# Gate rows ahead of the first projection's last chunk, their bias on VectorE, the sigmoid table loaded there, buffers cleared on GpSimd, and TensorE without a barrier into the attention

## The chip, the core and the metric

One program on one core of a Trainium2 chip (trn2). The metric is the device time of one execution in microseconds, the median of several; lower is better. Of the engines, PE is TensorE, ACT is ScalarE, DVE is VectorE, POOL is GpSimd, and SP is SyncE, which here only issues DMAs. ACT issues DMAs as well, on a queue of its own (q10; SP's is q1).

## What is computed

One layer of a hybrid encoder block: an adaptive norm of `x`, one combined input projection, a stick-breaking attention branch (8 heads of 64), a gated DeltaNet branch (4 heads of 128), sigmoid merge gates, an output projection and a gated residual. S = 1024 rows, D = 1024. The parts that the change touches:

```python
mod = silu(c) @ ada_w + ada_b
shift, scale, gate = split(mod, 3)
h = rms_norm(x, norm_g) * (1 + scale) + shift
p = h @ w_in                     # sb_q, sb_k, sb_v, sb_z, dn_*, merge_*
qa = rms_norm(heads(sb_q), sb_q_g); ka = rms_norm(heads(sb_k), sb_k_g); va = heads(sb_v)
o_sb = stick_breaking_attention(qa, ka, va) * silu(sb_z)
...
out = x + gate * (y @ w_out)
```

For a block of 128 queries, stick-breaking attention takes `keep = sigmoid(-z)` of the scores, a running product of `keep` from the diagonal back over the keys, and weighs differences of neighbouring value rows with it.

## The kernel before

All five engines run written-out instruction streams, ordered by semaphores. The program is a list of phases. At the end of phases 1 and 2 (and 3, but for TensorE) each engine drains, raises `phase_end` and waits until all five have (`end_phase`, L252): a barrier. Phase 1 is the first projection, phase 2 the attention.

**Phase 1** (`pe_1`, `act_1`, `dve_1`, `pool_1`, `sp_1`). 1536 columns of `w_in` (q, k, v of the attention) go in NCH = 6 chunks of 256, the last with 8 columns more. A chunk is 8 row tiles (ST); a tile is 24 matmuls, as each factor is split in a high and a low part and three of the four products are taken (`three`, L266 to L268). ACT copies every tile from PSUM to `rows` and raises `r_ok`. DVE sums squares for the norms of q (part 0) and k (part 1); ACT makes `y1` from them with Ln and Exp (L638, L639), the second time behind the copy of the last chunk's fourth tile; DVE then scales all eight row tiles (`normalize`, L663, L667), and makes the high part of a first weight tile `w3hl` of the next projection (L740), from which POOL makes the low part (L747). The per-channel gate of the residual: DVE sums `ada_w` weighted by silu(c) into `gacc` (128 x 1024), and a product with a matrix of ones sums over partitions and spreads the row over all of them; a second product adds the bias row `adab`. This stands behind the last chunk:

```python
for half in range(2):
    nc.tensor.matmul(bank(5 + half), ones[:], gacc[:, ...], start=True, stop=False)        # L619
    t = nc.tensor.matmul(bank(5 + half), ones[0:1, :], adab[0:1, ...], start=False, stop=True)   # L620
t.then_inc(gate_mm, 1)
```

ACT copies the result to `gate` (L641) as its last work of the phase.

**Phase 2** (`pe_2`, `act_2`, `dve_2`, `pool_2`, `sp_2`). PE first turns k and q of the first pair of heads (`turn(0)` to `turn(3)`, 16 transposes, L954), then works 24 matmuls of the next projection (`fill_2(-1)`, L758), then `scores(0)` and `scores(1)` (L971, L973). ACT casts the turned blocks (`high`, L1038) and DVE makes the low parts (`low`, L1091). The k half is copied by DMA to the other 64 partitions (`second_half`, the DMA `qk<-qk`, L924, two of them, semaphore `dup_ok`); `scores(0)` waits for it. SP writes the value rows to DRAM (`v_scratch<-rows`, L918, 2 MB) and, when they have landed, reads back the last row of each tile (`vE`, L929, `e_in`) and all rows shifted by one (`vsh`, L930, 2 MB, `v_in`). PE turns vE (L1014) between `scores(1)` and `scores(2)`, and DVE copies that to `vTe` (L1109) between scans 0 and 1. POOL takes `vsh - v` in four instructions (L1124, `dv_ok`), which the weighted sums (`values`, L1000) and later `high(4)` need.

The attention has 64 steps n, a query block of one head each, with the longest key range first: 1024, 1024, 896, 896, 768, 768, 640, 640, ... columns. A step is: scores on PE, `keep(n)` on ACT (sigmoid, L1045), `scan(n)` on DVE (the running product, L1098), transposes on PE (`flips`, L985), copies on ACT (L1053), and `values` on PE. PE's order is written out: `scores(0)`, `scores(1)`, vE's transposes, `scores(2)`, the 24 matmuls of `fill_2(0)`, `scores(3)`, `flips(0)`, and so on.

Of the kernel before, what the change touches and what calls it, by code (L numbers as in the profile page):

```python
# [26 lines left out]
P = 128  # L27
# [23 lines left out]
def hybrid_block(nc, x, c, ada_w, ada_b, norm_g, w_in, sb_q_g, sb_k_g, conv_w, dn_a_log, dn_dt_bias,  # L51
# [21 lines left out]
    with ctx:  # L73
# [213 lines left out]
        ss1_ok, y1_ok = sem("ss1_ok"), sem("y1_ok")  # L287
# [312 lines left out]

        def pe_1(pe):
            first_chunks(pe)
            for ch in range(2, NCH):
                pe.wait_ge(w1_hi, ch + 1)
                pe.wait_ge(w1_lo, ch + 1)
                for st in range(ST):
                    n = (ch - 1) * ST + st
                    pe.wait_ge(r_ok, n - 2 if ch == 2 and st < 4 else n - 3)
                    for kt in range(KT):
                        w = [t[:, kt, 0:width_1(ch)] for t in (high_of(ch), low_of(ch))]  # L610
                        t = three(bank(n % 4)[:, 0:width_1(ch)], hhi[:, kt, P * st:P * st + P],
                                  hlo[:, kt, P * st:P * st + P], w[0], w[1], kt == 0, kt == KT - 1)
                    t.then_inc(r_mm, 1)

            pe.wait_ge(r_ok, ST)
            pe.wait_ge(gacc_ok, 1)
            pe.wait_ge(par1_in, 80)
            for half in range(2):
                nc.tensor.matmul(bank(5 + half), ones[:], gacc[:, 512 * half:512 * half + 512], start=True, stop=False)  # L619
                t = nc.tensor.matmul(bank(5 + half), ones[0:1, :], adab[0:1, 512 * half:512 * half + 512],  # L620
                                     start=False, stop=True)
            t.then_inc(gate_mm, 1)

        def act_1(act):
# [4 lines left out]
            for n in range(ST, (NCH - 1) * ST):  # L629
                ch, st = n // ST + 1, n % ST  # L630
                act.wait_ge(r_mm, n + 1)
# [8 lines left out]
            act.wait_ge(gate_mm, 1)  # L640
            nc.scalar.copy(gate[:], psum[:, 5:7, :].rearrange("p a b -> p (a b)"))  # L641

        def dve_1(dve):
# [13 lines left out]
            def normalize(part):  # L657
# [3 lines left out]
                for st in range(ST):  # L661
                    v = rows[:, part, st].rearrange("p (h d) -> p h d", d=HD)
                    t = nc.vector.tensor_tensor(v, v, rstd1[:, st, :, None].to_broadcast([P, SBH, HD]), ALU.mult)  # L663
                    if part:

                        link(dve, dve_chain, t)
                        nc.vector.tensor_tensor(v, v, gain[:, 2, None, :].to_broadcast([P, SBH, HD]), ALU.mult)  # L667
# [12 lines left out]
            dve.drain().then_inc(gacc_ok, 1)  # L680
# [236 lines left out]
        def sp_2(sp):  # L917
            sp.dma_start(v_dram[1:1 + S].rearrange("(t p) n -> p t n", p=P), rows[:, 2]).then_inc(vd_out, 16)  # L918
# [28 lines left out]
        def pe_2(pe):  # L947
            def turn(u):

                part, half = TURNS[u % 4]  # L950
                if u >= 4:
                    pe.wait_ge(fl_ok, u - 1)
                for j in range(4):
# [4 lines left out]
            def scores(n):  # L958
                pair, qb, head = steps[n]
                if n % PER == 0:  # L960
                    pe.wait_ge(fl_ok, 4 * pair + 3)
                    pe.wait_ge(dup_ok, 32 * (pair + 1))
# [42 lines left out]

            for u in range(4):
                turn(u)
            fill_2(pe, -1)
            pe.wait_ge(c2_ok, 2)
# [18 lines left out]
        def act_2(act):  # L1028
            act.preload_act_table_set("sigmoid_and_others")
# [54 lines left out]
        def dve_2(dve):  # L1084
# [16 lines left out]
            nc.vector.memset(cast(qk[HD:P, 0, 2]), 0.0)  # L1101
            nc.vector.memset(floor[:, 0:S - P], 0.0).then_inc(c2_ok, 1)
# [15 lines left out]
        def pool_2(pool):  # L1118
            nc.gpsimd.memset(cast(qk[HD:P, 1, 2]), 0.0).then_inc(c2_ok, 1)
            pool.wait_ge(v_in, 16)  # L1120
            pool.wait_ge(c2_ok, 2)
# [896 lines left out]
        def run(eng, *phases):  # L2018

            for n, phase in enumerate(phases):  # L2020
                phase(eng)
                if n in (1, 2) or n == 3 and eng is not nc.tensor:
                    end_phase(eng, n)
                elif n == 3:
# [35 lines left out]
```

## Time and profile before

| | us |
|---|---|
| median of 3 runs | 1000.46 (998.68 to 1000.68) |
| profiled execution, its time | 1000.31 |
| its span in the trace | 998.4 |
| PE busy | 960.5 (96%) |
| DVE busy | 526.7 (53%) |
| ACT busy | 321.2 (32%) |
| POOL busy | 194.2 (19%) |

The trace is one execution, with times from the start of its span; 1.9 us of its time lie outside the span. Phase 1's last chunk ends at about 177 us, and phase 2 lasts from 182 to 338 us. TensorE's clock has two levels, 1.2 and 2.4 GHz; the views give the granted one as a share of the upper, and its mean over this execution is 0.987. In the chain of waits each step is the work, or the transfer, that released the next.

### The profile page before, as it was taken

The page shows a single profiled execution, that of the slowest core. Times are in us where ns is not written, and L with a number is a line of the kernel's source. Part 1 is how long each engine was busy: PE and PEld are TensorE (multiplying, and loading weights), DVE is VectorE, ACT ScalarE, POOL GpSimd, SP SyncE. Part 2 cuts the span into 40 slices and gives each one's busy share as a digit, 9 for nine tenths or more (in the row PEclk, how much of TensorE's full clock was granted, in tenths as well). Part 3 has the DMA queues.
Part 4 walks back from the last instruction along what each step waited for, and adds up shares of the span by engine and source line. Part 5 has one row for each costly group of instructions (what it writes and reads, how often), then busy time and mean ns, then how long its engine had stood idle before and what let it go on. Part 6 is the DMA issues. An engine that isn't in the chain of part 4 may idle for free.

```text
span 998.4 us, 14136 instructions
## 1 busy us (share of the span) xinstructions
PE 960.5 (96%) x5731; PEld 806.6 (81%) x5731; DVE 526.7 (53%) x763; ACT 321.2 (32%) x732; POOL 194.2 (19%) x96
## 2 busy tenths in 40 slices
PE   4999999999999899999999999999999989999998
PEld 3889999677777688888887888888888768787886
DVE  3776895689777245544233357123335456754422
ACT  7552111477876322112541111122322642110000
POOL 0001120160001011221222121100010026773000
PEclk9799999899999999999999999999999999999999
DMA  9851500611210211111312434512112773436231
GB/s 320 234 172 42 171 2 22 213 42 27 62 46 15 60 50 53 43 43 43 94 55 85 125 107 132 123 43 74 54 43 74 263 253 127 147 106 211 90 100 64
DMA packets 120587, 100.58 MB, mean 101 GB/s; under 512 B 18023, under 2 KB 100544, under 8 KB 120266
## 3 DMA queue, kind: packets, MB, share of 16 engines
q1 hardware_dynamic: 90218, 76.07, 25.3%
q10 hardware_dynamic: 30304, 23.60, 7.9%
q8 instruction: 46, 0.75, 0.3%
q14 instruction: 19, 0.16, 0.1%
HBM read 73.44 MB, written 24.12 MB: 98 GB/s over the span
## 4 chain that ended last, share of the span: by engine, by line
PE 77%; DVE 7%; DMA 6%; ACT 4%; POOL 3%; issue 2%; SPq 1%; ACTq 0%; DVEq 0%
PE psum L758 36%; PE psum L266 8%; PE psum L268 7%; PE psum L267 7%; DMA sg<-z_scratch 3%; DVE stick L1098 3%; PE psum L1000 3%; PE psum L985 2%; PE psum L971 1%; PE psum L1325 1%; ACT sg L1899 1%; POOL hlo L1928 1%; POOL sg L1937 1%; POOL w3hl L747 1%; PE psum L381 1%
## 5 line engine op out<-in xcount | busy, mean ns | idle before, releaser
L758 PE MATMUL psum<-hhi,w3hl 128*128 128x512 f32 x1120 | 370.5, 401 | 5.1 <-issue 2.3
L758 PEld LDWEIGHTS psum<-hhi,w3hl 128*128 128x128 f32 x1120 | 211.6, 189 | 50.9 <-issue 5.6
L758 PE MATMUL psum<-hlo,w3hl 128*128 128x512 f32 x560 | 219.2, 391 | 0.0
L747 POOL TENSOR_TENSOR w3hl<-w3raw,w3hl 128x1024 fp32r<-128x1024 f32 x43 | 104.6, 2432 | 510.3 <-DVE w3hl L740 510.3
L758 PEld LDWEIGHTS psum<-hlo,w3hl 128*128 128x128 f32 x560 | 106.1, 189 | 21.8 <-issue 1.9
L1098 DVE TENSOR_TENSOR_SCAN stick<-stick,floor 128x1024 f32<-128x1024 f32 (+7 forms) x64 | 94.2, 1510 | 24.5 <-ACT stick L1045 24.4
L266 PE MATMUL psum<-w1hi,hhi 128*128 128x256 f32 (+2 forms) x320 | 99.4, 311 | 0.0
L268 PE MATMUL psum<-w1hi,hlo 128*128 128x256 f32 (+2 forms) x320 | 98.3, 307 | 0.0
L267 PE MATMUL psum<-w1lo,hhi 128*128 128x256 f32 (+2 forms) x320 | 98.3, 307 | 0.0
L758 PE MATMUL psum<-ohi,w3hl 128*128 128x512 f32 x256 | 80.6, 395 | 3.3 <-issue 3.3
L740 DVE CAST w3hl<-w3raw 128x1024 fp32r<-128x1024 f32 x43 | 35.4, 822 | 72.2 <-DMA w3raw<-in_w_in 44.0
L842 ACT COPY zst<-psum 128x512 f32<-128x512 f32 x44 | 25.9, 589 | 130.2 <-PE psum L758 124.4
L268 PEld LDWEIGHTS psum<-w1hi,hlo 128*128 128x128 f32 x320 | 61.0, 191 | 3.2
L267 PEld LDWEIGHTS psum<-w1lo,hhi 128*128 128x128 f32 x320 | 61.3, 192 | 2.8
L266 PEld LDWEIGHTS psum<-w1hi,hhi 128*128 128x128 f32 x320 | 61.2, 191 | 2.8
L758 PEld LDWEIGHTS psum<-ohi,w3hl 128*128 128x128 f32 x256 | 48.8, 191 | 14.4 <-issue 4.1
L266 PE MATMUL psum<-w7hi,hhi 128*128 128x512 f32 x128 | 49.9, 390 | 1.2 <-POOL hlo L1928 1.2
L758 PE MATMUL psum<-olo,w3hl 128*128 128x512 f32 x128 | 50.4, 393 | 0.0
L268 PE MATMUL psum<-w7hi,hlo 128*128 128x512 f32 x128 | 49.8, 389 | 0.0
L267 PE MATMUL psum<-w7lo,hhi 128*128 128x512 f32 x128 | 49.8, 389 | 0.0
L1045 ACT ACTIVATE stick<-psum 128x1024 f32<-128x1024 f32 (+7 forms) x64 | 42.0, 658 | 20.5 <-PE psum L973 18.5
L1212 DVE SCALAR_TENSOR_TENSOR cacc<-xpad,paramT,cacc 128x1024 f32<-128x1024 f32 x36 | 46.2, 1285 | 1.3
(221 smaller groups left out, 1430.4 us busy)
## 6 DMA issues: line engine op xcount, KB each, us to landing
z_scratch<-zst ACTq DMA_DIRECT2D x44, 256.0 KB, 2.1
w3raw<-in_w_in ACTq DMA_DIRECT2D x20, 512.0 KB, 4.2
ada<-in_ada_w SPq DMA_DIRECT2D x16, 512.0 KB, 5.8
w3raw<-in_w_in SPq DMA_DIRECT2D x16, 512.0 KB, 4.0
sg<-z_scratch SPq DMA_DIRECT2D x8, 1024.0 KB, 5.1
xrow<-in_x SPq DMA_DIRECT2D x4, 1024.0 KB, 6.1
w1raw<-in_w_in SPq DMA_DIRECT2D x4, 1024.0 KB, 8.1
adag<-in_ada_w SPq DMA_DIRECT2D x8, 512.0 KB, 4.4
```

The source lines that it names most:

```text
L266: nc.tensor.matmul(out_, lh, rh, start=first, stop=False)
L267: nc.tensor.matmul(out_, lh, rl, start=False, stop=False)
L268: return nc.tensor.matmul(out_, ll, rh, start=False, stop=last)
L740: nc.vector.tensor_copy(weights(i)[0], w3raw[:]).then_inc(w3_hi, 1)
L747: nc.gpsimd.tensor_tensor(lo, w3raw[:], cast(hi), ALU.subtract).then_inc(w3_lo, 1)
L758: t = nc.tensor.matmul(out_, a[:, kt, :], moving[b][:, kt, 512 * half:512 * half + 512], start=(ends[0] and kt == k0 and m == 0), stop=(en ...
L842: nc.scalar.copy(zst[:, n // KT % 2], fill_bank(n // KT)).then_inc(zc_ok, 1)
L985: f = nc.tensor.transpose(t_cols(n, a)[:, P * (kb_ - 4 * a):P * (kb_ - 4 * a) + P], stick[:, n % NC, P * kb_:P * kb_ + P], ident[:, :])
L1000: v = nc.tensor.matmul(o_bank(m)[h0:h0 + HD, 0:P], rows[:, 2, kb_, P * pair + h0:P * pair + h0 + HD], wT_slots[tile_of[2 * m + head, a] % ...
L1045: nc.scalar.activation(stick[:, n % NC, 0:keys(n)], z_cols(n), ACT.Sigmoid, scale=-1.0).then_inc(keep_ok, 1)
L1098: nc.vector.tensor_tensor_scan(p_, p_, floor[:, S - keys(n):S][:, ::-1], 1.0, ALU.mult, ALU.max).then_inc(scan_ok, 1)
L1212: nc.vector.scalar_tensor_tensor(out=acc, in0=xpad[:, i % 2, k:k + S], scalar=tap[k], in1=acc, op0=ALU.mult, op1=ALU.add).then_inc(tap_ok, 1)
```

## The change

- **Gate rows.** The two matmuls with `gacc` stand in PE's stream ahead of the last chunk (`gate_rows`). The two with `adab` are gone: DVE adds the bias row to row 0 of `gacc`. ACT copies `gate` ahead of its copies of the last chunk.
- **Table.** ACT loads the sigmoid table behind the second Ln and Exp pair, not at the attention's start.
- **Value rows.** ACT's queue, not SP's, writes them to DRAM, first thing in phase 2.
- **Clearing.** Two buffers that DVE cleared at the attention's start (`qk[64:128, 0, 2]`, `floor`) are cleared by POOL ahead of the one that it cleared already.
- **TensorE** drains and raises `phase_end` behind phase 1 as before, and doesn't wait for the others. In the barrier's place stand a wait for the whole of `normalize(1)` (`n1_ok`) and for the first tile of the last chunk, and, ahead of `turn(2)`, one for all copies.

```diff
+        def gate_rows(pe):
+            pe.wait_ge(r_ok, ST)
+            pe.wait_ge(gacc_ok, 1)
+            for half in range(2):
+                t = nc.tensor.matmul(bank(5 + half), ones[:], gacc[:, 512 * half:512 * half + 512], start=True, stop=True)
+            t.then_inc(gate_mm, 1)
...
             for ch in range(2, NCH):
+                if ch == NCH - 1:
+                    gate_rows(pe)
...
-            pe.wait_ge(r_ok, ST)
-            pe.wait_ge(gacc_ok, 1)
-            pe.wait_ge(par1_in, 80)
-            for half in range(2):
-                nc.tensor.matmul(bank(5 + half), ones[:], gacc[:, 512 * half:512 * half + 512], start=True, stop=False)
-                t = nc.tensor.matmul(bank(5 + half), ones[0:1, :], adab[0:1, 512 * half:512 * half + 512],
-                                     start=False, stop=True)
-            t.then_inc(gate_mm, 1)
...
+                if ch == NCH - 1 and st == 0:
+                    act.wait_ge(gate_mm, 1)
+                    nc.scalar.copy(gate[:], psum[:, 5:7, :].rearrange("p a b -> p (a b)"))
...
+                    if n >= 4 * ST:
+                        act.preload_act_table_set("sigmoid_and_others")
-            act.wait_ge(gate_mm, 1)
-            nc.scalar.copy(gate[:], psum[:, 5:7, :].rearrange("p a b -> p (a b)"))
...
+                if part:
+                    t.then_inc(n1_ok, 1)
...
-            dve.drain().then_inc(gacc_ok, 1)
+            dve.wait_ge(par1_in, 80)
+            dve.wait_ge(gate_part, GG)
+            nc.vector.tensor_tensor(gacc[0:1, :], gacc[0:1, :], adab[0:1, :], ALU.add).then_inc(gacc_ok, 1)
...
         def sp_2(sp):
-            sp.dma_start(v_dram[1:1 + S].rearrange("(t p) n -> p t n", p=P), rows[:, 2]).then_inc(vd_out, 16)
...
+                elif u == 2:
+                    pe.wait_ge(r_ok, (NCH - 1) * ST)
...
+                if n == PER:
+                    pe.wait_ge(c2_ok, 3)
...
+            pe.wait_ge(n1_ok, 1)
+            pe.wait_ge(r_ok, (NCH - 2) * ST + 1)
             for u in range(4):
                 turn(u)
             fill_2(pe, -1)
-            pe.wait_ge(c2_ok, 2)
+            pe.wait_ge(c2_ok, 1)
...
         def act_2(act):
-            act.preload_act_table_set("sigmoid_and_others")
+            act.dma_start(v_dram[1:1 + S].rearrange("(t p) n -> p t n", p=P), rows[:, 2]).then_inc(vd_out, 16)
...
-            nc.vector.memset(cast(qk[HD:P, 0, 2]), 0.0)
-            nc.vector.memset(floor[:, 0:S - P], 0.0).then_inc(c2_ok, 1)
...
         def pool_2(pool):
+            nc.gpsimd.memset(cast(qk[HD:P, 0, 2]), 0.0).then_inc(c2_ok, 1)
+            pool.wait_ge(c2_ok, 1)
+            nc.gpsimd.memset(floor[:, 0:S - P], 0.0).then_inc(c2_ok, 1)
+            pool.wait_ge(c2_ok, 2)
             nc.gpsimd.memset(cast(qk[HD:P, 1, 2]), 0.0).then_inc(c2_ok, 1)
             pool.wait_ge(v_in, 16)
-            pool.wait_ge(c2_ok, 2)
+            pool.wait_ge(c2_ok, 3)
...
-                if n in (1, 2) or n == 3 and eng is not nc.tensor:
+                if n == 2 or n in (1, 3) and eng is not nc.tensor:
                     end_phase(eng, n)
-                elif n == 3:
+                elif n in (1, 3):
                     eng.drain().then_inc(phase_end, 1)
```

On PE, between the last chunk (L268 is its last matmul) and the attention's first transposes (L954), there stands before:

```order
L268 MATMUL psum<-w1hi,hlo 128x264
L619 MATMUL psum<-gacc,ones 128x512 [waits par1_in,gacc_ok,r_ok]
L620 MATMUL psum<-adab,ones 128x512
L619 MATMUL psum<-gacc,ones 128x512
L620 MATMUL psum<-adab,ones 128x512
L954 MATMUL psum<-ident,rows 128x128 [waits phase_end]
```

In the changed kernel the same place on PE reads (L963 are the transposes; the rows with `gacc`, now L606, stand 192 matmuls earlier):

```order
L268 MATMUL psum<-w1hi,hlo 128x264
L963 MATMUL psum<-ident,rows 128x128 [waits r_ok,n1_ok]
L963 MATMUL psum<-ident,rows 128x128 x7
L963 MATMUL psum<-ident,rows 128x128 [waits r_ok]
L963 MATMUL psum<-ident,rows 128x128 x7
```

The wait for the barrier has become one for the norm of k. On ACT, from the copy of the last tile to the attention's first casts (L1038), there stands before:

```order
L633 COPY ba<-psum 128x8 [waits r_mm]
L634 COPY rows<-psum 128x256
L641 COPY gate<-psum 128x1024 [waits gate_mm]
L1029 ACT_TABLE_LOAD [waits phase_end]
L1038 CAST qk<-psum 64x512 [waits a_q_mm]
```

The same place on ACT in the changed kernel (L1051 are the casts):

```order
L637 COPY ba<-psum 128x8 [waits r_mm]
L638 COPY rows<-psum 128x256
L1042 DMA v_scratch<-rows 128x8x512 [waits phase_end]
L1051 CAST qk<-psum 64x512 [waits a_q_mm]
L1051 CAST qk<-psum 64x512
```

The copy of `gate` has left the place ahead of the barrier, and between the barrier and the casts a DMA issue stands where the table load was. SP's stream behind the barrier now starts with the load of `floor`.

## Rows read from the trace of the kernel before

**Rows 1.** The page: busy time and share of the span by engine.

```profile
PE 960.5 (96%) x5731; PEld 806.6 (81%) x5731; DVE 526.7 (53%) x763; ACT 321.2 (32%) x732; POOL 194.2 (19%) x96
```

**Rows 2.** Chain of waits, 176 to 240 us: start, duration, what.

```profile
176.92 0.86 PE psum L619 x2
...
181.09 1.01 ACT gate L641
...
182.18 1.28 ACT L1029
...
185.88 6.38 DMA qk<-qk
...
192.39 0.47 PE psum L971
...
195.82 5.50 PE psum L758 x24
...
203.33 13.19 DVE stick L1098 x4
```

**Rows 3.** Timeline of ACT: start, duration, instruction, idle time before and its releaser.

```profile
168.26 0.17 ACT L633 COPY ba<-psum 128x8 f32<-128x8 f32 x1 [1.92 <-PE psum L268]
```

**Rows 4.** Timeline of DVE, 140 to 215 us.

```profile
166.37 0.20 DVE L258 TENSOR_SCALAR nt<-ss 128x64 f32<-128x64 f32 x1 [9.98 <-ACT y L639]
177.62 0.69 DVE L667 TENSOR_TENSOR rows<-rows,gain 128x512 f32<-128x512 f32 x1
185.32 5.59 DVE L1091 TENSOR_TENSOR qk<-psum,qk 64x512 fp32r<-64x512 f32 x8
197.17 4.20 DVE L1098 TENSOR_TENSOR_SCAN stick<-stick,floor 128x1024 f32<-128x1024 f32 x2
```

**Rows 5.** Timeline of POOL, 140 to 216 us.

```profile
142.09 5.12 POOL L538 TENSOR_TENSOR w1lo<-w1raw,w1hi 128x2112 fp32r<-128x2112 f32 x1 [31.53 <-DVE w1hi L532]
179.06 2.34 POOL L747 TENSOR_TENSOR w3hl<-w3raw,w3hl 128x1024 fp32r<-128x1024 f32 x1 [31.86 <-DVE w3hl L740]
182.18 1.80 POOL L1119 MEMSET qk<- 64x2048 f32 x1 [0.77 <-ACTq L252]
199.50 15.66 POOL L1124 TENSOR_TENSOR rows<-vsh,rows 128x1024 f32<-128x1024 f32 x4 [15.52 <-DMA vsh<-v_scratch]
```

**Rows 6.** Timeline of SP: DMA issues at the attention's start.

```profile
182.15 0.39 SPq L918 DMA_DIRECT2D v_scratch<-rows  x1
189.63 0.30 SPq L929 DMA_DIRECT2D vE<-v_scratch  x1
189.97 0.50 SPq L930 DMA_DIRECT2D vsh<-v_scratch  x1
```

**Rows 7.** The issues of L924 (`qk<-qk`): landing times over the program.

```profile
DMA to landing us min/median/max: 2.9/3.1/6.5
```

**Rows 8.** Groups of scans on DVE, 230 to 252 us: busy, mean ns.

```profile
L1098 DVE TENSOR_TENSOR_SCAN stick<-stick,floor 128x896 f32<-128x896 f32 x2 | 3.9, 1992 | 0.0
L1098 DVE TENSOR_TENSOR_SCAN stick<-stick,floor 128x768 f32<-128x768 f32 x2 | 3.4, 1726 | 0.0
L1098 DVE TENSOR_TENSOR_SCAN stick<-stick,floor 128x640 f32<-128x640 f32 x2 | 3.0, 1475 | 0.5 <-ACT stick L1045 0.5
```

**Rows 9.** Windows of PE: length, busy time, granted clock, DMA share, GB/s.

```profile
18.00:20.00 2.00, 2.00 (x11) 1.00 1.10 348
21.00:25.00 4.00, 4.00 (x39) 1.00 1.17 310
```

**Rows 10.** Windows of PE around the first projection's end, same columns.

```profile
176.00:180.50 4.50, 4.50 (x16) 1.00 0.00 0
180.75:187.25 6.50, 5.38 (x21) 0.50 0.67 241
```

**Rows 11.** Timeline of PE: the last of `fill_2(-1)`, and vE's transposes.

```profile
191.79 0.39 PE L758 MATMUL psum<-hhi,w3hl 128*128 128x512 f32 x1
...
194.39 0.41 PE L1014 MATMUL psum<-ident,vE 8*128 8x8 f32 x4
```

More of the change, by code:

```diff
@@ L286, in hybrid_block @@
         gate_part, gacc_ok, gate_mm = sem("gate_part"), sem("gacc_ok"), sem("gate_mm")
-        ss1_ok, y1_ok = sem("ss1_ok"), sem("y1_ok")
+        ss1_ok, y1_ok, n1_ok = sem("ss1_ok"), sem("y1_ok"), sem("n1_ok")
         const_v = const.rearrange("p (n q) -> p n q", q=P)
@@ L666, in normalize @@
                         link(dve, dve_chain, t)
-                        nc.vector.tensor_tensor(v, v, gain[:, 2, None, :].to_broadcast([P, SBH, HD]), ALU.mult)
+                        t = nc.vector.tensor_tensor(v, v, gain[:, 2, None, :].to_broadcast([P, SBH, HD]), ALU.mult)
+                if part:
+                    t.then_inc(n1_ok, 1)
             high_1(dve, 2)
```

## Prediction

> **What bounds the kernel now.** I read the page first: PE is busy for 960.5 us of 998.4 [rows 1], so time is lost or won only where PE stands still, or where PE is delayed by work that isn't hidden. The change touches one such place, the passage from the first projection to the attention. The chain of waits [rows 2] shows who holds it there: the gate matmuls from 176.92 to 181.09, ACT's copy of `gate` to 182.10, the barrier, the table load to 183.46, ACT's casts, the transfer `qk<-qk` to 192.26, and `scores(0)` at 192.39. The reader is to see two things more. First, PE's clock: it is granted whole up to 180.5 and half from then to 187.25 [rows 10], after four us of gate matmuls (two passes of about 0.52 us each for 512 columns, against 0.23 a matmul in the 24 at 195.82, [rows 2]). Yet `fill_2(-1)` is done at about 192.0 [rows 11], 0.2 us before the transfer: both end nearly together, and taking away one alone gives 0.2 us. Second, the chain from 203.33 to 216.52 is four scans on DVE, 13.19 us [rows 2]. Alone, scans of these widths take 1.99, 1.73, 1.73 and 1.48 us [rows 8], in sum 6.9.
>
> **The stretch behind the start.** Those four scans lie beside POOL's four subtractions, 199.50 to 215.16 [rows 5]. A POOL instruction of the same size took 2.34 us alone (L747 at 179.06), but these take 3.9 each. From the end of scan 2 at 201.37 (197.17 + 4.20, [rows 4]) to the end of scan 6 at 216.52 it is 15.15 us; less 6.9 for the scans, 8.2 remain, 2.06 for each of the four subtractions. So the two engines don't overlap here, they take turns, and the stretch lasts as long as the sum of both. The Trainium skill says why, in "GPSIMD Engine Reference", Key points: GpSimd shares its SBUF interfaces with VectorE, with contention when VectorE's instruction has two SBUF inputs; a scan of `stick` with `floor` has two. The trace agrees with it, 3.9 us beside scans against 2.34 alone. The stretch can start when scan 2 is done and `vsh` has landed; now `vsh` is there at 199.50 and scan 2 ends at 201.37, so the scan decides, with 1.9 us to spare. What the change is worth is read from these two times. They are followed step by step below.
>
> **Gate rows.** Four matmuls take (181.09 - 176.92), 1.04 each [rows 2]. Two go: PE has 2.1 us less in sum. The other two move ahead of the last chunk, so all of it comes 2.1 later: its end at 179.0 instead of 176.9, and its fourth tile, behind which ACT makes `y1`, too: the first instruction that uses it at 168.5 instead of 166.37 [rows 4]. DVE had idled 9.98 us for it, so `normalize(1)` shifts whole, its end from 178.31 to 180.4, and so do the cast behind it and POOL's L747: 181.2 to 183.5 instead of 181.40 [rows 5]. ACT's copy of `gate`, 1.01, falls into its idle time between tiles. DVE's addition on one row: 1024 elements, at most twice the 0.69 of a 512-element instruction [rows 4], so 0.7 to 1.4, less a drain; the idle 9.98 us cover it, and the last weights, made by 147.2 [rows 5], have 6.5 us until PE wants them (the last chunk's 8 tiles at 2.90 end at 176.92, so it starts at 153.7). Cost nothing; without that cover 1.4.
>
> **The barrier** now waits for POOL, not for ACT: 183.55 instead of 182.15. It comes 1.4 later for all but PE.
>
> **ACT.** The table load, 1.28 [rows 2], moves into 1.92 us of idle time ahead of a copy [rows 3]: free. In its place the issue of the value rows' store, 0.39 on SP [rows 6]. Casts start at 183.6 + 0.4 = 184.0, against 183.5 behind the table load: 0.5 later. Behind that issue stand all eight casts, so DVE's low parts and both `qk<-qk` wait for it: the second is issued at 186.4 instead of 185.88 [rows 2].
>
> **PE.** Last chunk to 179.0, idle until `n1_ok` at 180.4, 16 transposes to 182.2 (39 transposes in 4.00 us [rows 9]), idle until POOL's part of the weights at 183.5, then 24 matmuls, 5.5 us as at 195.82 [rows 2]: done at 189.1, against 192.0. This is 2.9 us won, if the clock stays up. "TensorE: Matmul & The Clock Gate", Part 4, of the Trainium skill says that transposes don't count as busy for the clock gate; by it PE would look idle from 179.0 to 183.6 and the clock would fall. This trace says otherwise: with nothing but transposes on PE, 11 ran in 2.00 us up to 20, and 39 in 4.00 after 21 [rows 9], that is, they brought the clock up. With a clock at half for 6.5 us as before [rows 10] the 24 matmuls would end near 192.3.
>
> **DVE and POOL at the start.** DVE's clearing held the low parts until 185.32 [rows 4]; now the first casts do, until 185.2. The third block is done at 189.4. POOL clears in three pieces after 183.6: 1.80, about 0.8, 1.80 [rows 5]; `floor` is ready at 186.3, needed by scan 0 after 190. Free.
>
> **`scores(0)`.** It waits for the fill (189.1), the low parts (189.4) and the transfer. Before, that transfer stood behind the 2 MB store in one queue and took 6.38 us; with the queue to itself it takes 3.1 [rows 7]. Now the store is on ACT's queue, started 1.4 later, and both queues use the same engines, which were filled already (DMA share 0.67 over a window that starts before the store, [rows 10]). From both sides: 186.4 + 3.1 = 189.5, and 186.4 + 6.4 = 192.8. I take 191.5, two thirds of the way, as the store is in full flow. Scan 2 ended 8.98 us after `scores(0)` began: 200.5 (198.5 to 201.8).
>
> **`vsh`.** From the store's issue to vE's 7.48, to `vsh`'s 0.34, to POOL's start 9.53: 17.35 [rows 5, 6]. The same bytes move in that time after the change, only in another order (the two `qk<-qk` within the store, not between it and `vsh`). So 183.55 + 17.35 = 200.9. Bounds: `vsh` waited until 192.26 for the transfers ahead of it, 2.3 us; without that 198.6, with it on both sides 203.2.
>
> **vE.** It landed before 194.39, as PE didn't wait [rows 11]; its issue comes 1.4 to 3.7 later. I take a wait of up to 1.5 us ahead of `scores(2)`. What it delays is scan 3, and while DVE waits POOL takes its next turn: with two subtractions ahead of scan 3 the pair is busy until 205.1. So it costs nothing up to there, and 1 us for each us beyond.
>
> **Sum.** The stretch starts at the later of 200.5 and 200.9, against 201.37: -0.5 us. 2.9 us won on PE, 1.28 on ACT and 1.4 lost at the barrier all vanish in it. From the profiled execution, 1000.31 - 0.5 = 999.8; the median lies 0.15 above that execution, so **1000.0 us**.
>
> **Rivals.** (a) *The start moves as a whole, faster.* The transfer is alone at 189.5 and `vsh` lands at 198.6: the stretch starts at 198.6, 2.8 us earlier: 997.7. For it: `vsh` has nothing ahead of it in its queue. Against: the store begins 1.4 later, and the bytes are the same. 0.17. (b) *The gate rows pull the clock down within the last chunk, slower.* Before, it fell behind four of these matmuls. If two are enough, PE works at half clock, as for 6.5 us from 180.75 on [rows 10]. Each us at half clock delays the chunk by 0.5, and `y1`, the barrier and `vsh` with it: 3.3 for 6.5 us: 1003.3. It turns the sign past 0.5 and shows in the measurement past 5 us of half clock. For it: their passes take 2.3 times as long as the others. Against: there are 2.1 us of them, with dense work on both sides. 0.06. (c) *The store, cut up by the two transfers, lands late:* `vsh` at 203.2, past scan 2; the stretch ends 1.8 later: 1002.3. Past 0.2% only with a late vE. 0.07. (d) *Nothing but the order changes:* my forecast, 0.70.
>
> **Numbers.** 0.2% of 1000 is 2.0 us, about what a measurement here tells from no change. The range 998.2 to 1002.2 holds (d), (c) mostly and the near part of (a). Faster by over 0.2%: 0.17; within: 0.72; slower: 0.11.
>
> **What would show it.** In the trace after: last chunk's end near 179.0; POOL's L747 ending last before the barrier, 183.5; PE idle twice, 1.4 and 1.3 us, around the transposes; the transfer landing between 189.5 and 192.8; POOL's first subtraction starting near 201; scans and subtractions still taking turns, and scan 6 ending near 216.0. Wrong, if scan 6 ends before 214.5 or after 218.5, or if the stretch behind it doesn't keep what it was given.

## The result, and the profile after

The changed kernel takes 1003.02 us in the median of 11 runs (1000.93 to 1005.61); the kernel before took 1000.46 beside it (11 runs, 998.06 to 1001.61). The ratio is 1.0028, with a 95% interval of 1.0018 to 1.0038: slower by 1.8 to 3.8 us. I had forecast 1000.0, range 998.2 to 1002.2.

The profiled execution of after took 1005.61 us, with a span of 1003.7. Of the 5.3 us between the two profiled executions only a part is the change's. I cut each trace at one event that lies ahead of everything the change touches: ScalarE's copy of the last tile of the fifth chunk, the last row before the final chunk (for each kernel the timeline of ACT, then the one of DVE at the passage's end; before first, then after).

```profile
153.76 0.37 ACT L634 COPY rows<-psum 128x256 f32<-128x256 f32 x1 [2.46 <-PE psum L268]
229.51 0.67 DVE L740 CAST rowsr<-w3raw 128x1024 fp32r<-128x1024 f32 x1
```

```profile
156.01 0.37 ACT L638 COPY rows<-psum 128x256 f32<-128x256 f32 x1 [2.47 <-PE psum L268]
234.04 0.67 DVE L748 CAST rowsr<-w3raw 128x1024 fp32r<-128x1024 f32 x1
```

After is 2.25 us late before the changed code begins. That is no effect of the change: the third experiment's kernel is the same program up to there, and has this copy at 153.46. From the copy to DVE's cast of the next weights (L740, now L748) I call it the **passage**: 75.75 us before, 78.04 after (by rows before rounding), so +2.29. That agrees with the interval of the medians. Behind the passage it is 768.9 us against 769.7 (2.25, 2.29 and 0.8 make the 5.3); over all kernels of this study that rest lies between 766.3 and 770.3 with no relation to the edits that I can see, so I read edits by the passage and by the medians, never by one execution's time. All times "in the passage" below count from that copy's start.

The chain of waits of after, 170 to 235 us (start, duration, what):

```profile
183.04 2.45 POOLq L252
185.50 0.42 ACTq L1042
185.97 0.58 ACT qk L1051
...
188.38 6.97 DMA qk<-qk
195.48 0.47 PE psum L982
...
200.39 5.48 PE psum L766 x24
205.90 0.60 ACT rows L841
206.93 0.93 ACT stick L1058
207.88 11.05 DVE stick L1111 x3
```

The reader is to see that the chain has the old shape [rows 2]: barrier, ScalarE's casts, the transfer `qk<-qk` (6.97 us where it was 6.38), the scores, 24 matmuls, scans. The table load is gone from it, the gate matmuls too, and it is still longer. Queues and engines at the same place (timelines of SP, ACT, POOL, DVE and PE of after):

```profile
187.17 2.11 SPq L931 DMA_DIRECT2D qk<-qk  x2
193.65 0.30 SPq L936 DMA_DIRECT2D vE<-v_scratch  x1
193.99 0.79 SPq L937 DMA_DIRECT2D vsh<-v_scratch  x1
...
191.91 0.37 ACTq L814 DMA_DIRECT2D z_scratch<-rows  x1
...
183.06 2.34 POOL L755 TENSOR_TENSOR w3hl<-w3raw,w3hl 128x1024 fp32r<-128x1024 f32 x1 [32.36 <-DVE w3hl L748]
204.75 12.55 POOL L1139 TENSOR_TENSOR rows<-vsh,rows 128x1024 f32<-128x1024 f32 x4 [14.60 <-DMA vsh<-v_scratch]
...
170.34 0.20 DVE L258 TENSOR_SCALAR nt<-ss 128x64 f32<-128x64 f32 x1 [10.45 <-ACT y L643]
200.43 4.20 DVE L1111 TENSOR_TENSOR_SCAN stick<-stick,floor 128x1024 f32<-128x1024 f32 x2
207.88 12.42 DVE L1111 TENSOR_TENSOR_SCAN stick<-stick,floor 128x896 f32<-128x896 f32 x4 [3.25 <-ACT stick L1058]
...
190.87 0.39 PE L766 MATMUL psum<-hhi,w3hl 128*128 128x512 f32 x1
195.48 0.47 PE L982 MATMUL psum<-qk 128*128 128x512 f32 x1 [4.23 <-DMA qk<-qk]
```

PE has done the fill at 191.26 and stands still for 4.23 us; scan 3 starts 3.25 us behind scan 2, where it had been 1.96 (203.33 less 201.37, [rows 2, 4]). The windows of PE in after (length, busy time by engine, then granted clock, DMA share, GB/s):

```profile
188.00:191.00 3.00, 3.00 (x15) 2.36 (x13) 2.91 (x5) 2.69 (x5) 2.10 (x2) 1.00 1.06 386
191.50:195.30 3.80, 0.00 (x0) 0.00 (x0) 1.38 (x2) 0.38 (x1) 0.00 (x0) 1.00 1.01 272
196.40:199.80 3.40, 3.40 (x12) 2.35 (x11) 1.80 (x1) 2.05 (x2) 0.00 (x0) 0.51 0.85 248
200.00:203.00 3.00, 3.00 (x16) 2.50 (x15) 2.97 (x4) 0.92 (x1) 0.00 (x0) 1.00 1.06 396
```

Full clock in the fill, nothing at all while it waits, then 0.51 under the first scores, some 0.9 us after PE has begun again. Before, the phase at half clock lay under the end of the gate matmuls, the transposes and the first 2 us of the fill [rows 10], where the barrier and the transfer hid it (experiment 8 shows how well); now it lies on the path.

### The profile page after: what moved, and what is told of

It reads as the page before. It is cut to its first block, busy times and chain, and to the rows that moved or that the text cites. A ratio compares the mean times of both kernels' runs of the same rounds, so it can differ in the third digit from the quotient of the medians.

```text
span 1003.7 us, 14132 instructions
## 1 busy us (share of the span) xinstructions
PE 959.0 (96%) x5727; PEld 806.7 (80%) x5727; DVE 524.4 (52%) x762; ACT 321.8 (32%) x732; POOL 193.6 (19%) x98
## 4 chain that ended last, share of the span: by engine, by line
PE 76%; DVE 8%; DMA 6%; ACT 4%; POOL 3%; issue 2%; SPq 1%; ACTq 0%; POOLq 0%; DVEq 0%
PE psum L766 36%; PE psum L266 7%; PE psum L267 7%; PE psum L268 7%; DMA sg<-z_scratch 3%; PE psum L1011 3%; DVE stick L1111 3%; PE psum L996 2%; PE psum L982 2%; PE psum L1340 1%; ACT sg L1914 1%; POOL hlo L1943 1%; PE psum L381 1%; POOL sg L1952 1%; PE psum L984 1%
## 5 line engine op out<-in xcount | busy, mean ns | idle before, releaser
L755 POOL TENSOR_TENSOR w3hl<-w3raw,w3hl 128x1024 fp32r<-128x1024 f32 x43 | 104.6, 2432 | 513.4 <-DVE w3hl L748 513.4
L1111 DVE TENSOR_TENSOR_SCAN stick<-stick,floor 128x1024 f32<-128x1024 f32 (+7 forms) x64 | 93.4, 1499 | 27.1 <-ACT stick L1058 26.9
L268 PE MATMUL psum<-w1hi,hlo 128*128 128x256 f32 (+2 forms) x320 | 98.3, 307 | 0.0
L748 DVE CAST w3hl<-w3raw 128x1024 fp32r<-128x1024 f32 x43 | 34.3, 798 | 72.9 <-DMA w3raw<-in_w_in 42.8
L268 PEld LDWEIGHTS psum<-w1hi,hlo 128*128 128x128 f32 x320 | 61.0, 191 | 3.1
L268 PE MATMUL psum<-w7hi,hlo 128*128 128x512 f32 x128 | 49.8, 389 | 0.0
```

The costliest lines, as they stand in the source:

```text
L268: return nc.tensor.matmul(out_, ll, rh, start=False, stop=last)
L748: nc.vector.tensor_copy(weights(i)[0], w3raw[:]).then_inc(w3_hi, 1)
L755: nc.gpsimd.tensor_tensor(lo, w3raw[:], cast(hi), ALU.subtract).then_inc(w3_lo, 1)
L1111: nc.vector.tensor_tensor_scan(p_, p_, floor[:, S - keys(n):S][:, ::-1], 1.0, ALU.mult, ALU.max).then_inc(scan_ok, 1)
```

## Experiments

Eleven kernels, in three sets (1 to 4, 5 to 8, 9 to 11); each set shares its runs of the kernel before, whose medians are 1000.08, 1000.84 and 1000.75 us, and each ratio is to those of its own set. The columns: when ScalarE or SP issued the value rows' store and when the second `qk<-qk` transfer landed, both in us from the cut; scan 3's start less scan 2's end; the length of the passage; where in the passage a phase at half clock began, and how long it was. In 6, 9 and 11 the store is that of the second half of the columns. Each trace is one execution.

| kernel | store issued | landed | gap to scan 3 | passage | half clock | median, ratio to before, 95% |
|---|---|---|---|---|---|---|
| before | 28.4 | 38.5 | 1.96 | 75.75 | 26.9 for 6.8 | 1000.46 |
| after | 29.5 | 39.3 | 3.25 | 78.04 | 40.3 for 3.4 | 1003.02, 1.0028 (1.0018 to 1.0038) |
| 1 gate rows behind | 27.8 | 37.5 | 3.76 | 76.57 | 36.9 for 6.8 | 1000.39, 1.0010 (0.9997 to 1.0023) |
| 2 `y1` early | 25.5 | 35.1 | 3.40 | 73.77 | 36.6 for 3.4 | 998.07, 0.9983 (0.9970 to 0.9997) |
| 3 store on SP | 29.5 | 39.5 | 3.06 | 78.14 | 40.3 for 3.4 | 1003.36, 1.0040 (1.0023 to 1.0057) |
| 4 PE busy | 29.5 | 39.2 | 1.96 | 77.06 | none | 1002.25, 1.0020 (1.0008 to 1.0031) |
| 5 gate rows in idle time | 23.7 | 33.4 | 1.96 | 71.47 | none | 995.89, 0.9959 (0.9947 to 0.9972) |
| 6 half a store | 25.5 | 32.5 | 1.96 | 69.72 | none | 994.91, 0.9947 (0.9932 to 0.9962) |
| 7 gate rows alone | 29.5 | 39.7 | 1.96 | 76.96 | 29.9 for 3.4 | 1000.81, 1.0013 (1.0003 to 1.0023) |
| 8 small subtractions | 28.3 | 38.3 | 1.96 | 74.28 | none | 1000.02, 0.9999 (0.9989 to 1.0009) |
| 9 combination | 23.8 | 30.9 | 0 | 70.21 | none | 995.89, 0.9952 (0.9935 to 0.9969) |
| 10 as 1, PE busy | 27.8 | 37.5 | 1.95 | 75.56 | none | 999.04, 0.9989 (0.9976 to 1.0001) |
| 11 fill later | 25.5 | 32.5 | 0 | 69.71 | none | 993.97, 0.9933 (0.9915 to 0.9951) |

One reading joins the rows of this table. Call **start** the later of two moments, the end of scan 2 and GpSimd's first subtraction. From the start to the end of scan 6 it is 15.1 to 15.6 us in every kernel but 8. From there to the passage's end it is 13.0 us; in the four kernels whose clock fell under the scores (after, 1, 2, 3) it is 13.7, and only 8 and 9 differ (17.6 and 14.9). The start is at 47.6 before, 48.7 in after, 48.8 in 7, 48.7 in 4, 47.2 in 10 and 41.6 in 6 and 11. So the 2.29 us of the change are 1.13 in the start, 0.41 in the stretch and 0.75 behind it.

**1. The gate rows back behind the last chunk,** all else as after.

```diff
-                if ch == NCH - 1:
-                    gate_rows(pe)
...
+            gate_rows(pe)
...
-                if ch == NCH - 1 and st == 0:
-                    act.wait_ge(gate_mm, 1)
-                    nc.scalar.copy(gate[:], psum[:, 5:7, :].rearrange("p a b -> p (a b)"))
...
+            act.wait_ge(gate_mm, 1)
+            nc.scalar.copy(gate[:], psum[:, 5:7, :].rearrange("p a b -> p (a b)")).then_inc(gate_ok, 1)
```

> The changed kernel, but its two gate matmuls and ACT's copy of gate stand behind the last chunk again (ahead of the attention's second turn, which waits for that copy). I call the passage the time from ACT's copy of the fifth chunk's last tile to DVE's cast of rowsr: 75.75 us before, 78.06 after the change. Theory A (the gate rows push back the last chunk, so the norm of k, POOL's part of the weights and the barrier come late, and the store, the casts and the transfer with them): the barrier comes 1.7 us earlier than after the change, the passage is 76.3 and the time 1001.3. Theory B (PE's new idle time ahead of scores(0) lets the clock fall, which costs 1.5 us): the idle time stays, passage 77.5 or more. Theory C (the store on ACT's queue is the fault, because it holds the casts and then stands in the way of the transfers): nothing of it changes, passage 77.5 to 78, time 1002.5 or more.

The passage is 1.47 us shorter than in after, the store issued 1.7 earlier. But the passage is still 0.82 longer than before, and the late phase at half clock is there, twice as long. So there is more than one cost.

**2. The norm's inputs early:** ScalarE's Ln, Exp and table load behind the first tile of the last chunk, not its fourth.

```diff
-                if n in (2 * ST + 7, 4 * ST + 3):
+                if n in (2 * ST + 7, 4 * ST):
```

> The changed kernel, with ACT's second Ln and Exp pair and the table load behind the first tile of the last chunk, not the fourth: 8.7 us earlier. Theory A: DVE and POOL are done before the last chunk ends, so the barrier opens with ACT's last copy, about 3.8 us earlier than after the change, PE goes on with the transposes without a gap, and the passage falls to 74 to 75, the time to 999 to 1000. Theory C: the start moves too, but the transfer still lands some 7 us behind its issue. Theory B: idle time of PE ahead of scores(0) of 4 us stays, as all that PE and the transfer wait for moves alike, so the clock can still fall there and the passage stays above 75.5.

The barrier opens 4.0 us earlier and the passage ends 4.27 earlier. What comes behind the barrier moves with it, nearly one for one. This kernel is a little faster than before (0.03% to 0.3%), with the gate rows in front of the chunk.

**3. The store on SP's queue again,** ahead of the floor's load.

```diff
+            sp.dma_start(v_dram[1:1 + S].rearrange("(t p) n -> p t n", p=P), rows[:, 2]).then_inc(vd_out, 16)
...
-            act.dma_start(v_dram[1:1 + S].rearrange("(t p) n -> p t n", p=P), rows[:, 2]).then_inc(vd_out, 16)
```

> The changed kernel, with the store of the value rows back on SP's queue, ahead of the load of floor. Theory C: the passage falls back to 76 to 76.5 and the time to 1000.8 or less. Theory A: only the 0.42 us of the issue ahead of the casts go, the transfer lands as late as before behind the store, passage 77.6, time 1002.5. Theory B: the idle time of PE is 0.4 shorter, no more than 0.5 us.

No gain: 78.14 against 78.04. In two queues or in one, the transfer lands 9.8 to 10.1 us behind the store's issue. The theory that the second queue costs falls.

**4. TensorE kept busy while it waits:** 16 matmuls with an unused result behind the fill.

```diff
             fill_2(pe, -1)
+            for i in range(16):
+                nc.tensor.matmul(bank(3), weights(0)[0][:, i % KT, :], hhi[:, i % KT, 0:512], start=True, stop=True)
```

> The changed kernel with 16 more matmuls on PE behind fill_2(-1), into a bank that scores(1) overwrites: 3.7 us of work whose result is not used, in the 4.2 us in which PE had idled. Theory B: the clock stays up through scores(0) to scores(2), scan 3 can start 1.5 us earlier, passage 76.5 and time 1001.4. Theory A and C: scores(0) still waits for the transfer, and the clock's fall is hidden behind POOL's subtractions, so passage 77.8 to 78 and time 1003.

The timeline of PE and that of DVE in this kernel, and a window of it over the wait:

```profile
191.26 3.79 PE L1023 MATMUL psum<-hhi,w3hl 128*128 128x512 f32 x16
195.52 0.47 PE L982 MATMUL psum<-qk 128*128 128x512 f32 x1 [0.47 <-DMA qk<-qk]
...
206.47 16.26 DVE L1113 TENSOR_TENSOR_SCAN stick<-stick,floor 128x896 f32<-128x896 f32 x6 [1.96 <-ACT stick L1060]
```

```profile
191.50:195.40 3.90, 3.55 (x16) 2.62 (x14) 1.53 (x3) 0.55 (x1) 0.00 (x0) 1.00 1.02 282
```

The scores start at the same moment as in after (195.52 and 195.48 in executions that stand 0.17 apart), the clock stays whole, the gap ahead of scan 3 is 1.96 again, and the passage 0.98 shorter. That is the price of the clock's fall; the medians move the same way (1002.25 against 1003.02), but their intervals overlap. Scan 3 starts 1.58 earlier in the passage, but the scans give 1.34 back at once, since more of POOL's subtractions lie beside them (four scans 13.78 us against 12.42 in after); the other 0.74 comes later, where DVE waits 0.46 us for ScalarE's casts of the next pair of heads (L1053) and not 1.20.

**5. The gate rows in TensorE's idle time:** the second kernel, with the two matmuls behind the fill, in two other banks, and their copy behind the fill's.

```diff
-                if ch == NCH - 1:
-                    gate_rows(pe)
...
             fill_2(pe, -1)
+            pe.wait_ge(fl_ok, 2)
+            gate_rows(pe)
```

> The second experiment with the gate rows taken off the last chunk altogether: the two matmuls on [1,512] halves stand behind the fill's rest, where PE is idle until the vsh rows land, and ScalarE's gate copy behind its fill copies. If the gate rows in the last chunk cost what they take there (1.74 us), because everything behind the chunk hangs on its end: store issue at 23.7 us from the fifth chunk's last copy (25.48 in the second experiment), transfer lands 9.7 us behind it at 33.4, passage 72.0 us against 73.8, time about 996.3 us. If instead the 25.48 us is set by something other than TensorE (ScalarE's copies, the norm chain on VectorE), the store issue stays at about 25.3 and the time at 998.

As expected: the store is issued at 23.7 and the transfer lands at 33.4, both to 0.1 us, the passage is 0.5 us shorter than expected, and the time is 0.4% below before's. 1.74 us off the chunk give 2.30 in the passage; the clock's fall has gone as well, with most of PE's wait filled by real work (0.95 us of it are left, up to the landing of `qk<-qk`; it isn't `vsh` that PE waits for there, as I had written).

**6. Half of the store early:** the second kernel, with columns 0 to 255 of the value rows stored on SP's queue during the last chunk.

```diff
+            sp.wait_ge(r_ok, (NCH - 2) * ST)
+            sp.dma_start(v_dram[1:1 + S, 0:256].rearrange("(t p) n -> p t n", p=P), rows[:, 2, :, 0:256]).then_inc(vd_out, 16)
...
-            act.dma_start(v_dram[1:1 + S].rearrange("(t p) n -> p t n", p=P), rows[:, 2]).then_inc(vd_out, 16)
+            act.dma_start(v_dram[1:1 + S, 256:512].rearrange("(t p) n -> p t n", p=P), rows[:, 2, :, 256:512]).then_inc(vd_out, 16)
```

> The second experiment with columns 0 to 255 of the value rows stored during the last chunk on SP's queue, and only columns 256 to 511 at the start of the attention. Theory 1: the projected rows' transfer lands 9.7 us behind the store's issue because the store's bytes go ahead of it on the same engines; then with half of the bytes it lands 2 to 4 us earlier behind the issue (6 to 7.7 us), unless descriptors rather than bytes count, the scores begin as much earlier, POOL's vsh wait (18.8 us behind the issue) shrinks as well, and the passage is 2 to 3 us shorter: 71 to 72 us, time 995.5 to 996. Theory 2: the 9.7 us is issue and descriptor work of the transfer itself or of its queue; then it lands at 9.7 us as before and the time stays at 998.

Here is who has the DMA engines, in after from the first `qk<-qk` issue (187.17) on, and in this kernel from the same issue (182.88) on: the queues' view, with packets, MB, and share of 16 engines (q1 is SP's, q10 ScalarE's).

```profile
q10 hardware_dynamic: 805, 1.65, 105.7%
```

```profile
q10 hardware_dynamic: 794, 0.81, 108.9%
```

The first is 187.2 to 191.4 us of after, the second 182.9 to 185.0 of this kernel; in neither stretch is there one packet of q1. In after, the transfer's first packet starts at 191.9, 4.7 us behind its issue, when 0.17 of the store's 2.10 MB are left; here at 185.3, 2.4 behind. The packets are about as many in both stretches (805 in 4.2 us, 794 in 2.1) and half as large here, so it is the bytes that count and not the packets. The transfer lands 7.0 us behind the store's issue and not 9.7 (4.1 us from its own issue, and not 6.8), and PE runs on from the fill to the scores without a pause: the passage is 4.05 us shorter than in the second kernel, 1 more than expected, because the clock's fall is gone too. "DMA: Bandwidth & Descriptors", Queues, rings and completion order, of the Trainium skill says that each DMA engine takes turns between its queues at the granularity of a packet. By that rule a small transfer in a second queue would be served soon; these traces don't show it, they show it served when nine tenths or more of the bytes ahead of it had gone. With the queues exchanged it looks the same: before, ScalarE's 256 KB store of projected rows (L806), issued 2.9 us behind the 2 MB load `vsh` in SP's queue, lands 7.2 us behind its issue and 0.6 behind `vsh`, where the median of that line's 48 transfers is 2.2.

**7. The gate rows alone:** the kernel before, with the two matmuls ahead of the last chunk, the bias on DVE, and the copy; nothing else of the change.

```diff
+                if ch == NCH - 1:
+                    gate_rows(pe)
...
-            dve.drain().then_inc(gacc_ok, 1)
+            nc.vector.tensor_tensor(gacc[0:1, :], gacc[0:1, :], adab[0:1, :], ALU.add).then_inc(gacc_ok, 1)
```

> The kernel before with one part of the change alone: the gate rows ahead of the last chunk, with the bias added on VectorE and the copy on ScalarE ahead of the chunk; the TensorE barrier, the table load, the memsets and the store's queue stay. If it is this part that costs (all of the chunk's end, norm chain, barrier and store 1.1 to 1.7 us later, the projected rows' transfer with them): barrier at 29.5 to 30.1 us from the fifth chunk's last copy (28.42 before), passage 76.9 to 77.5 us against 75.75, time 1001.5 to 1002.2. If it is the other parts (queue of the store, removed barrier wait, the clock's fall ahead of the scores): the passage stays at 75.8 and the time at 1000.5.

Barrier 1.13 later (29.55 against 28.42), passage 1.21 longer, ratio 1.0013. All of it is in the start, here the end of scan 2 (48.8 against 47.6). The part that was to take 2.1 us off TensorE costs 1.2 us by itself.

**8. Small subtractions:** the kernel before, GpSimd subtracting 2 of the 128 columns of each head pair. The kernel leaves out the rest of the differences, so its output is not the layer's.

> The kernel before in which GpSimd subtracts 2 columns of the 128 of each head pair only; the rest of the differences of the value rows is left out. If VectorE's scans and GpSimd's subtractions hold each other up (13.19 us for four scans of 2.0 to 2.2 us alone), the four scans from the fourth on take 7 to 9 us instead of 13.2 and the passage is 3 to 5 us shorter, if nothing else is the bound there: time about 996 us. If the scans wait for ScalarE or TensorE instead, the four scans' stretch stays at 12 to 13 us and the time within 1 us of 1000.5.

The timeline of DVE in this kernel:

```profile
196.80 4.20 DVE L1098 TENSOR_TENSOR_SCAN stick<-stick,floor 128x1024 f32<-128x1024 f32 x2
202.95 5.32 DVE L1098 TENSOR_TENSOR_SCAN stick<-stick,floor 128x896 f32<-128x896 f32 x3 [1.96 <-ACT stick L1045]
208.81 1.49 DVE L1098 TENSOR_TENSOR_SCAN stick<-stick,floor 128x640 f32<-128x640 f32 x1 [0.53 <-ACT stick L1045]
211.45 1.49 DVE L1098 TENSOR_TENSOR_SCAN stick<-stick,floor 128x640 f32<-128x640 f32 x1 [1.16 <-ACT stick L1045]
```

Scans 3 to 6 take 7.35 us with a wait of 0.53 in them, and without the wait 6.8, as they take alone [rows 8]; so it is GpSimd that stretches them to 13.19 [rows 2]. But 5.8 us off this stretch give 1.47 in the passage and nothing that the medians show: from scan 6 on DVE waits for `keep` on ScalarE (L1045), and the chain of waits there runs on TensorE. The bound behind it is near. This trace shows one thing more. Up to the subtractions the program is that of before, yet there is no phase at half clock in it. PE has done the fill 2.7 us earlier (35.7 against 38.4), and the scores begin only 0.2 earlier: that is how little the phase cost where it lay before.

**10. Both costs out:** the first and the fourth experiment together.

> Both suspected costs of the change taken out of it at once: the gate rows stand behind the last chunk again, as in the first experiment, and 16 matmuls whose result nobody uses stand behind the fill's rest, as in the fourth. If the loss is the sum of the two costs (gate rows in front +1.2 us, late half-clock phase +1.0 us, as the seventh and the fourth experiment give them), no half-clock phase begins behind the fill, scan 3 starts 1.95 us behind scan 2's end and not 3.8, and the passage is 74.9 to 75.6 us, at or under the 75.75 of before; time 999 to 1000.5 us. If something else in the change costs as well, the passage stays at 76.3 or more and the time over 1001.

75.56 us, 0.19 under before: what is left of the change costs nothing. Against experiment 1 it is 1.01 shorter, a second price for the clock's fall beside the 0.98. The sum closes: 1.21 for the gate rows (7) and 0.98 for the clock (4) are 2.19 of the 2.29 us. But what is left wins nothing either, though the first scores begin 1.0 us earlier than before (37.6 against 38.6): GpSimd's first subtraction, at 47.2, is 1.5 later than before and now behind scan 2's end (46.6), so the start moves by 0.4 and not by 1.0. The timeline of POOL in this kernel:

```profile
202.73 13.97 POOL L1142 TENSOR_TENSOR rows<-vsh,rows 128x1024 f32<-128x1024 f32 x4 [14.83 <-DMA vsh<-v_scratch]
```

**11 and 9. Past the sixth kernel.** In every kernel so far scan 3 waited for the fill's second half tile. 11 moves it behind `scores(3)`; 9 does so too, and takes the gate rows off the chunk into the loop behind `scores(2)`.

```diff
-        fill_at = {-1: 8, 0: 8}
+        fill_at = {-1: 8, 1: 8}
```

> The sixth experiment with the second half tile of the fill (24 matmuls, 5.5 us on TensorE) one step later: behind scores(3) and not ahead of them, with its copy on ScalarE. In all seven kernels so far scan 3 starts 1.95 us or more behind scan 2's end, and the chain of waits goes through these 24 matmuls, ScalarE's copy of them and keep(3). If they are what scan 3 waits for, the scans follow one another without that idle time (0.1 us), and the passage is about 1.8 us shorter: 67.9 us against 69.72, time about 993. If the flips and value products behind them come late instead and VectorE waits there, or if GpSimd's subtractions set the pace (they run 40.3 to 55.4 us), the passage stays at 69 to 70 and the time at 995.

> The combination: half of the value rows stored early, the norm's inputs and table load early, the gate rows off the last chunk and off TensorE's way to the first scores (they stand behind scores(2), in two banks that are free there, and their copy behind keep(2)), and the fill's second half tile behind scores(3). The chunk ends 1.74 us earlier than in the sixth experiment; if the first scores wait for TensorE alone there (fill's rest ends, scores(0) follow), they begin 1.7 us earlier: 30.9 us from the fifth chunk's last copy, and the passage is 1.7 us shorter than in the kernel with the later fill, some 66.2 us, time 991 to 992. If the projected rows' transfer comes to be the bound, the gain is under 1 us; if the gate rows in the loop push keep(2) or keep(3) back, the gain is taken back at scan 2 or 3.

The shorter passage that both expectations put first doesn't come; in 11 it is the last alternative, that GpSimd's subtractions set the pace. The gap ahead of scan 3 is gone in both, and in 9 the first scan is 1.6 us earlier than in 6 (33.4 against 35.0), but the passage is 69.71 and 70.21 against 69.72. The timelines of DVE and POOL in 11, and its chain of waits, show where the 2 us went:

```profile
190.88 22.92 DVE L1113 TENSOR_TENSOR_SCAN stick<-stick,floor 128x1024 f32<-128x1024 f32 x9
...
194.05 14.79 POOL L1141 TENSOR_TENSOR rows<-vsh,rows 128x1024 f32<-128x1024 f32 x4 [10.53 <-DMA vsh<-v_scratch]
...
199.22 10.98 DVE stick L1113 x3
210.24 0.77 PE psum L998 x5
```

The scans follow one another without a pause, and scan 6 ends where it does in 6 (56.7 in the passage). From the start, 41.6 in both, it is 15.1 us in both: the subtractions lie beside the scans, the two engines take turns, and the time in which DVE had idled goes to them. An earlier scan 3 is worth nothing as long as the start stays, as the prediction's rule said. In 9 the start is 1.6 us earlier (40.0), and so is scan 6's end nearly (55.4), but from there it is 14.9 us to the cast and not 13.0. From the 24 matmuls of the fill on its chain of waits runs almost wholly on TensorE, and DVE waits 2.85 us ahead of scan 4, whose scores stand behind them. The sixth kernel and 11 are the fastest, 0.5% and 0.7% under before, with intervals that overlap.

## Why the prediction was wrong, step by step

- **Gate rows: right in direction.** The last chunk's end came 1.74 later and not 2.1 (ScalarE's last copy of it ends at 25.37 against 23.63 in the passage): that is what the two matmuls take there. The 1.04 each was the mean of four, the last 0.4 us of them at half clock. The chain `y1`, `normalize(1)`, cast, L755 shifted whole, as said: 170.34 is 14.33 in the passage, against 12.61. DVE's bias and ScalarE's copy and table load cost nothing, as said.
- **Barrier: right.** It opens 1.1 later (29.5 in the passage, behind POOL's L755, which ends at 29.39; it had been at 28.4), forecast 1.4. Casts 0.24 later, forecast 0.5.
- **PE's two pauses and the fill: right.** Pauses of 1.47 and 1.22, forecast 1.4 and 1.3; the fill done at 35.25 in the passage, forecast 35.3. The clock stayed whole through the 16 transposes and the fill. The rows that I took for it show 1.00 in both stretches, the slower one too [rows 9]: they show a whole clock beside transposes, and not, as I wrote, that transposes brought it up.
- **The transfer: the first step that failed.** I took 191.5 (37.7 in the passage) with bounds 35.7 to 39.0; it landed at 39.3, outside. I bounded its time from its own issue, by an idle queue (3.1) and by the old 6.38, and thought that a second queue would let it in between. (Two thirds of the way between the bounds would have been 191.7, and no row gave the two thirds.) What holds is one number from another event: it lands 9.6 to 10.2 us behind the issue of the 2 MB store, in one queue (before, 3, 7, 8) or two (after, 1, 2, 4, 5, 10), and 7.0 to 7.2 behind the issue of 1 MB (6, 9, 11). In before's trace it could have been read: 38.5 less 28.4. By it, the store 1.1 later makes the scores 0.9 later, and the 2.9 us won on PE (3.2 measured) can't count.
- **The clock under the scores: the step that was missing.** I asked whether the clock falls ahead of the fill, not what PE does once the fill is done early. This term stood at nothing in the sum. I had it idle for 191.5 less 189.1, 2.4 us, and it was 4.2. The granted clock then fell to half for 3.4 us; it costs 0.98 (4).
- **`vsh`: mis-sized.** Forecast 17.35 behind the store's issue, measured 19.25 (204.75 less 185.50): 48.74 in the passage and not 47.1. Its issue came 8.49 behind the store's, and not 7.82 [rows 6]; its flight was 10.7 us, not 9.5. The store of the fill's first half tile (191.91) now stands ahead of it; before it was issued at 192.83, behind. No run tries that alone, but all thirteen traces divide by it: where that store is issued ahead of `vsh` (after, 1 to 5, 10), `vsh` lands 10.6 to 11.0 us behind its issue, and where it is issued behind (before, 6 to 9, 11), 9.5 to 9.9.
- **The rule for the stretch's start held.** It starts at the later of scan 2's end (48.62) and the first subtraction (48.74): +1.1, forecast -0.5. Both came 1.6 to 1.9 us later than forecast, the one with the transfer, the other with `vsh`; either would have moved the start. Scans and subtractions do take turns (8, 11). But the stretch took 15.55 and not 15.14, and behind it there is less slack than I gave it: TensorE is close behind (8, 9), and what it loses at half clock comes out 0.74 us later.
- **A late scan 3.** "It costs nothing up to there" was wrong. The limit of 205.1, 51.3 in the passage, was for a first subtraction at 47.1; with the measured 48.74 and two subtractions alone, 2.4 us each, it is 53.5. Scan 3, at 51.87, lay within it, and the fall of the clock that made it late still cost 1.0 us (4): 0.24 in the stretch, 0.74 behind it.
- **Rivals.** (b) had the sign and a clock at half, but in another place: none fell in the gate rows. (c), `vsh` late, was near in time (1002.3) by luck. `vsh` was late, but in after it comes only 0.1 us behind scan 2's end; it costs 0.4 in 4 (48.73 against 48.33) and 0.65 in 10 (47.24 against 46.59), where without it scan 2's end would be the start, and nothing in 7. No rival said that the store's issue sets the transfer, whatever the queue.

In sum: forecast -0.5 in the passage, measured +2.3. 1.2 of it is what the gate rows delay, the store above all (7), and 1.0 is the clock (4). The 0.5 to be won by the earlier scores the transfer never let through.

## What to carry to other kernels

Work taken off an engine is worth nothing if half of it is moved ahead of what everybody waits for: here four matmuls became two, the two moved ahead of the last chunk, and the passage grew by 1.2 us (7); out of the chunk and in a pause (5 against 2) they left it 2.3 us shorter. Ask for a transfer which bytes are ahead of it on the DMA engines, in any queue, and count from their issue. Where two engines take turns, look for the moment from which both can work: only that moment, and the sum of their work, move the end. And when a step gets faster in front of a transfer, its engine waits longer there; on TensorE look what clock it comes back with.

## What the runs showed of the hardware

- A transfer of 256 KB in a second queue got no packet through for 4.7 us while a 2 MB store had all 16 engines (share 1.06); with half the bytes, in as many packets, it began after 2.4 us. 1 MB less is 2.7 us at the 393 GB/s of that stretch, and the transfer landed 2.7 us earlier behind the store's issue (7.0 in 6, 9.7 in 2).
- In after, PE idle for 4.23 us and then busy for 0.9 was followed by 3.4 us at half clock; in 7, where it waits 4.61 us behind the chunk for the barrier, half clock came 0.4 us after the wait. With 16 plain matmuls in the gap (4, 10), or the two gate matmuls (5), it stayed whole. In 3 and 2 the phase came as in after; in 1 it was 6.8 us long, with PE working through 6.1 of it. What decides between 3.4 and 6.8 stays open, and so does how sure the fall is: in 2 a wait of 2.72 us ahead of the scores was followed by one, in 8 a wait of 2.67 wasn't. And 8 is the same program as before up to its subtractions, and shows no half clock where before had 6.8 us of it.
- GpSimd's subtraction of 128 x 1024 took 3.9 us beside scans and 2.34 alone, and four scans took 13.19 us instead of 7.35 (8). Alone, the four scans are 6.9 us and the four subtractions 9.4; together they took 15.1 to 15.6 from the start, whatever the idle time between scans: nearly the sum.
